# A hybrid diffusion step on one core: expert rows turned elsewhere, the choice of experts inside scoring, half of the early sums on VectorE

## The reference

```python
def peer_ffn(h, wq, subkeys, u_tab, v_tab):
    ...
        q = (xt @ wq).reshape(PEER_CHUNK, PEER_HEADS, 2, PEER_HALF)
        sc = jnp.einsum('thpd,hpnd->thpn', q, subkeys).astype(jnp.float32)
        s_top, i_top = lax.top_k(sc, PEER_TOPK)
        cand = (s_top[:, :, 0, :, None] + s_top[:, :, 1, None, :]).reshape(PEER_CHUNK, PEER_HEADS, PEER_TOPK * PEER_TOPK)
        cidx = (i_top[:, :, 0, :, None] * PEER_NKEYS + i_top[:, :, 1, None, :]).reshape(PEER_CHUNK, PEER_HEADS, PEER_TOPK * PEER_TOPK)
        f_s, f_i = lax.top_k(cand, PEER_TOPK)
        e = jnp.take_along_axis(cidx, f_i, axis=-1)
        g = jax.nn.softmax(f_s, axis=-1).astype(xt.dtype)
        act = jax.nn.gelu(jnp.einsum('thkd,td->thk', u_tab[e], xt))
        return jnp.einsum('thk,thkd->td', g * act, v_tab[e])
```

## Time and profile before

| | us |
|---|---|
| Median of 3 runs | 3889.42 (3873.55 to 3904.28) |
| The profiled execution: its time, its span | 3899.92, 3898.1 |
| begin | 142.6 |
| project, att p (layer 0) | 153.6, 32.7 |
| rwkv p (layers 0, 1) | 160.6, 158.5 |
| score p (layers 0, 1) | 84.9, 92.5 |
| choose (layers 0, 1) | 31.0, 37.8 |
| att s, rwkv s, output s, score s (layer 0) | 105.6, 268.4, 84.8, 113.8 |
| exp (layers 0, 1) | 778.0, 737.9 |
| PE, DVE, ACT, POOL busy | 73%, 52%, 29%, 42% |
| DMA | 318 GB/s over the span |

### The profile page before, as it was taken

The page is one execution under the profiler, slowest core; times in us unless marked ns, Lnnn a source line. Parts: engine busy times, 40 slices in busy tenths (PEclk is TensorE's granted clock), DMA queues, the critical chain, the costliest instruction groups (busy, mean ns, idle before and its releaser), DMA issues. The chain is left out here.

```text
span 3898.1 us, 41250 instructions
## 1 busy us (share of the span) xinstructions
PE 2855.5 (73%) x13182; PEld 1768.7 (45%) x13182; DVE 2010.4 (52%) x5134; ACT 1112.1 (29%) x3048; POOL 1652.5 (42%) x1598
## 2 busy tenths in 40 slices
PE   5685775599776788888758675866996857777775
PEld 3584664356554233333228565843664622222221
DVE  1113337577567744444552234566765695445555
ACT  2444432332231211111124444433223212111111
POOL 0000002455334777777720000043643367777774
PEclk7897966799888999999979797767997999999998
DMA  9896972578877999999979798765987589999997
GB/s 386 327 361 237 365 275 100 210 254 296 313 249 248 362 410 410 411 410 409 409 290 348 253 360 315 251 245 188 327 294 275 189 318 362 384 392 409 406 408 280
DMA packets 332008, 1241.14 MB, mean 318 GB/s; under 512 B 41098, under 2 KB 45834, under 8 KB 316434
## 3 DMA queue, kind: packets, MB, share of 16 engines
q0 software_dynamic: 221184, 805.40, 54.5%
q10 hardware_dynamic: 75616, 276.96, 19.1%
q1 hardware_dynamic: 34996, 156.14, 10.6%
HBM read 1095.72 MB, written 142.64 MB: 318 GB/s over the span
## 5 line engine op out<-in xcount | busy, mean ns | idle before, releaser
L461 PE MATMUL acc<-more,rows 128*128 128x512 f32 x1712 | 820.8, 612 | 192.1 <-ACT rows L447 179.6
L423 DVE CUSTOM_DVE_ANT_0 rows<-rows,fetch_h_tok 128x1024 f32<-128x1024 f32 x536 | 655.0, 1223 | 437.9 <-DMA rows<-u_rows,fetch_eid 435.4
L402 POOL DMA_INDIRECT rows<-u_rows,fetch_eid x536 | 560.3, 1045 | 302.0 <-issue 155.5
L409 POOL DMA_INDIRECT more<-in_v,fetch_eid x428 | 452.6, 1057 | 386.9 <-PE acc L461 288.4
L441 ACT ACTIVATE fetch_gel<-fetch_dot 128x1 f32<-128x1 f32 x768 | 155.5, 203 | 1607.7 <-DVE fetch_dot L423 1593.2
L461 PEld LDWEIGHTS acc<-more,rows 128*128 128x128 f32 x1712 | 305.2, 192 | 638.7 <-issue 386.5
L461 PE MATMUL acc<-extra,rows 128*128 128x512 f32 x928 | 447.1, 609 | 145.5 <-ACT rows L447 130.8
L423 DVE CUSTOM_DVE_ANT_0 extra<-extra,fetch_h_tok 128x1024 f32<-128x1024 f32 x232 | 284.2, 1225 | 297.3 <-DMA extra<-u_rows,fetch_eid 297.0
L315 PE MATMUL rows_bank<-ident,rows 128*128 128x128 f32 x2048 | 301.7, 296 | 133.6 <-ACT rows L330 128.0
L330 ACT COPY rows<-rows_bank 128x512 f32<-128x512 f32 x512 | 276.3, 589 | 285.4 <-DMA u_rows<-rows 167.3
L461 PEld LDWEIGHTS acc<-extra,rows 128*128 128x128 f32 x928 | 160.2, 189 | 427.0 <-DMA extra<-in_v,fetch_eid 271.0
(11 more groups left out here) (918 smaller groups left out, 3827.0 us busy)
## 6 DMA issues: line engine op xcount, KB each, us to landing
rows<-in_u ACTq DMA_DIRECT2D x256, 512.0 KB, 6.4
u_rows<-rows ACTq DMA_DIRECT2D x256, 512.0 KB, 6.3
ring<-in_w_ada SPq DMA_DIRECT2D x48, 1024.0 KB, 8.1
ring<-in_wq SPq DMA_DIRECT2D x32, 1024.0 KB, 7.0
ring<-in_w_in SPq DMA_DIRECT2D x20, 1024.0 KB, 8.5
ring<-in_w_out SPq DMA_DIRECT2D x16, 1024.0 KB, 9.1
rows<-u_rows,fetch_eid POOLq DMA_INDIRECT x536, 6.6
more<-in_v,fetch_eid POOLq DMA_INDIRECT x428, 6.6
```

The costliest lines, as they stand in the source:

```text
L402: c.nc.gpsimd.indirect_dma_start(f.u[b], None, u_rows, bass.IndirectOffsetOnAxis(f.eid[:, t, k:k + 1], 0)).then_inc(c.landed_u[b], 16)
L409: c.nc.gpsimd.indirect_dma_start(f.v[b], None, v_rows, bass.IndirectOffsetOnAxis(f.eid[:, t, k:k + 1], 0)).then_inc(c.landed_v[b], 16)
L423: V.tensor_tensor_reduce(u, u, f.h_tok[:, t, :], 1.0, 0.0, ALU.mult, ALU.add, f.dot[:, n:n + 1]).then_inc(f.dots, 1)
L461: ins = c.nc.tensor.matmul(f.acc[2 * t + h][:, :], f.diag[:, n % DIAGS, :], f.v[f.place[n]][:, 512 * h:512 * h + 512], start=(k == 0), sto ...
```

## The change

Five things are changed.

1. No rows are turned in begin. `Turns_of` is 4 for grams, 2 for chunks and 3 for scan in place of 2, 1 and 2, so rwkv p turns 60 rows in each layer (46 before), and all 128 are turned when score p ends. Before, layer 0 had 18 rows in begin, 11 in score p and none in choose; layer 1 had 16 in score p and 13 in choose. Now score p has 15 in both.
2. `select` takes a range of heads. For the prompt it runs inside score p behind every second piece, for two heads at a time; choose keeps the last store of the rows, the exponential and the shares.
3. Of the slots below 114, every odd one (57 per layer) is summed on DVE into `summed`. ACT makes no diagonal for it, PE no product, and POOL's wait for its V buffer is on the sum's semaphore `added`. finish adds `summed` to `acc` for tile 0, with one operation more.
4. Blocks end without GpSimd's drain, and `clear` clears ranges of semaphores.
5. In exp, SP issues b_ada and w_ada first, and `load_for_norm` only when the samples' experts are chosen, since `select` there uses its buffer.

```diff
+BESIDE = 114
 class Turns_of:
-    begin, project, scores, values, grams, level, chunks, scan, out, q = 1, 2, 1, 1, 2, 3, 1, 2, 2, 1
+    project, scores, values, grams, level, chunks, scan, out, q = 2, 1, 1, 2, 4, 1, 2, 3, 1
...
 def clear(nc, sems):
-    for s in sems:
-        nc.sync.sem_clear(s)
-    nc.all_engine_barrier()
+    numbers = sorted(s.num for s in sems)
+    start = numbers[0]
+    for n, after in zip(numbers, numbers[1:] + [None]):
+        if after != n + 1:
+            nc.sync.sem_clear(range(start, n + 1))
+            start = after
+    nc.all_engine_barrier(sem_only=True)
...
+    f.by_vector = [n < BESIDE and n % 2 == 1 for n in range(STEPS)]
+    f.rank = [sum(1 for m in range(n + 1) if f.by_vector[m] == f.by_vector[n]) for n in range(STEPS)]
...
-                pool.wait_ge(f.slot_done, f.before[n] + 1)
+                m = f.before[n]
+                pool.wait_ge(f.added if f.by_vector[m] else f.slot_done, f.rank[m])
...
+        n = step - LAG
+        if 0 <= n < STEPS and f.by_vector[n]:
+            dve.wait_ge(c.landed_v[f.place[n]], f.count[n])
+            dve.wait_ge(f.weighted, n + 1)
+            if f.rank[n] == 1:
+                V.tensor_scalar(f.summed[:, :], f.v[f.place[n]], f.w[:, n:n + 1], None, ALU.mult).then_inc(f.added, 1)
+            else:
+                dve.wait_ge(f.added, f.rank[n] - 1)
+                V.scalar_tensor_tensor(f.summed[:, :], f.v[f.place[n]], f.w[:, n:n + 1], f.summed[:, :], ALU.mult, ALU.add).then_inc(f.added, 1)
...
-        if 0 <= n < STEPS:
+        if 0 <= n < STEPS and not f.by_vector[n]:
             t, k = divmod(n, SLOTS_OF_TOKEN)
             pe.wait_ge(c.landed_v[f.place[n]], f.count[n])
-            pe.wait_ge(f.diag_done, n + 1)
+            pe.wait_ge(f.diag_done, f.rank[n])
...
                 for m in range(TILES, N_ADA // PAIR):
                     ada_pair_copy(c, s, act, rows, m)
-                    rows_act(c, act, PAIR * Turns_of.begin)
...
                     ada_pair_product(c, s, pe, rows, piece_full, m)
-                    if m >= TILES:
-                        rows_pe(c, pe, PAIR * Turns_of.begin)
...
-        with nc.Block() as block:
+        with nc.Block(no_gpsimd_drain=True) as block:
...
+TOGETHER = 2
...
+                    if q is PROMPT and (m + 1) % TOGETHER == 0:
+                        if m + 1 == TOGETHER:
+                            dve.wait_ge(f.iota_in, 16)
+                        select(c, link, 0, lambda: None, spares, pick, m + 1 - TOGETHER, m + 1)
...
-def select(c, link, t, between, spares, pick):
+def select(c, link, t, between, spares, pick, first=0, end=PH):
...
-                dve.wait_ge(f.iota_in, 16)
-                select(c, link, 0, lambda: None, spares, pick)
                 rest_of_shares(c, dve, link, 0)
...
-                load_for_norm(c, l, sp, c.late_in, late, 1, "ln2")
                 if not last:
                     sp.dma_start(rows_mod[0:1, :], dram["b_ada"][l + 1:l + 2]).then_inc(S["bias_in"], 16)
...
                         fill_slot(c, sp, l, AT_ADA + n)
+                sp.wait_ge(f.routed, 2 * TILES)
+                load_for_norm(c, l, sp, c.late_in, late, 1, "ln2")
...
+                        if t == 0:
+                            ins = nc.vector.tensor_tensor(part[:, t, cols], c.fetch.acc[h][:, :], c.fetch.summed[:, cols], ALU.add)
...
+                    if t == 0:
+                        link(nc.vector.tensor_tensor(part[:, t, :], part[:, t, :], gates[:, 0, :], ALU.mult))
```

More of the change, by code:

```diff
@@ L38 @@
 WINDOW = 120
+BESIDE = 114
 DIAGS = 8
 class Turns_of:
-    begin, project, scores, values, grams, level, chunks, scan, out, q = 1, 2, 1, 1, 2, 3, 1, 2, 2, 1
+    project, scores, values, grams, level, chunks, scan, out, q = 2, 1, 1, 2, 4, 1, 2, 3, 1
 class Fetches_of:
-    begin, project, scores, values, grams, level, chunks, scan, out, q = 0, 0, 2, 2, 2, 3, 2, 2, 4, 1
+    scores, values, grams, level, chunks, scan, out, q = 2, 2, 2, 3, 2, 2, 4, 1
 SLOTS = 4
@@ L1865, in select @@
     V.scalar_tensor_tensor(rows_of[:, :, 1, :], halves[:, :, 1, :], float(NK), oddf, ALU.mult, ALU.add)
-    tops = f.top[:, t, :, :].rearrange("p (h two) k -> p h two k", two=2)
-    half0, half1, long = tops[:, :, 0, :], tops[:, :, 1, :], [P, PH, SHORT, TOPK]
+    tops = f.top[:, t, 2 * first:2 * end, :].rearrange("p (h two) k -> p h two k", two=2)
+    half0, half1, long = tops[:, :, 0, :], tops[:, :, 1, :], [P, heads, SHORT, TOPK]
     V.tensor_tensor(cand[:, :, 0:LONG_ROWS].rearrange("p h (a b) -> p h a b", a=SHORT),
@@ L1877, in select @@
         part = slice(8 * r8, 8 * r8 + 8)
-        for h in range(PH):
+        for h in range(heads):
             ins = V.max(best[:, h, part], cand[:, h, :])
@@ L1889, in select @@
     flat = pos.rearrange("p h k -> p (h k)")
-    V.tensor_tensor(f.share[:, t, :].rearrange("p (h k) -> p h k", h=PH), best[:, :, :],
-                    best[:, :, 0:1].to_broadcast([P, PH, TOPK]), ALU.subtract).then_inc(f.exp_asked, 1)
+    ins = V.tensor_tensor(f.share[:, t, ours].rearrange("p (h k) -> p h k", h=heads), best[:, :, :],
+                    best[:, :, 0:1].to_broadcast([P, heads, TOPK]), ALU.subtract)
+    if end == PH:
+        ins.then_inc(f.exp_asked, 1)
     V.tensor_copy(posf[:, :], flat)
```

71 lines of the change are left out of this document (39 added, 32 removed).

## The result

The changed kernel takes 3922.46 us (median of 9 runs, 3910.35 to 3929.99), the kernel before 3888.45 in the same comparison (9 runs). The ratio is 1.0092, 95% interval 1.0066 to 1.0117. I had forecast 3838 us.

What follows compares the result with a forecast made beforehand. Limits were taken by stage: transfers in begin and mid rwkv p, PE in score p, DVE in choose. Terms -40.6 + 52 - 10 - 22 - 14 - 26 + 8.6 = -52 took 3889.4 to 3838 us; range 3785 to 3885.

Steps and rivals of the forecast that it cites:

- Part 5, sums: Slots summed on VectorE instead of PE, mainly in the levels of rwkv s: -13 us a layer, -26 in all.
- DVE takes PE's place, and 0.8 us a level are left: Solve level in rwkv s: PE's 10.51 us become 7.9, DVE needs 9.7, so 0.8 of 2.6 us is gained.
- Att s runs at POOL's pace: 0: In att s POOL sets the pace, so the sums there change nothing: 0 us.
- The slower rival: Sums land on the path, each adding its 1.225 us: +140 for -26, 4003 us; chance 8%.
- Part 2, rows: Fourteen more rows in each rwkv p at 1.85 us a row, between 15 and 36 us: +52 for two layers.
- Part 3, choice: Choice inside score p: 9.8 us per two heads, stage bound by DVE, 118 us with choose; sum -10.
- Part 4, boundaries: Between stages: fewer semaphore clears give -22 us, GpSimd's drain left out behind att s gives -14.
- A drain left out can't cost: Stage ends: leaving out GpSimd's drain gives -14 us, or 0 if the hole is another wait.
- Part 6, exp: Exp and finish: about 0 in exp of layer 0, +6 in layer 1, 1.3 a layer in finish; sum +8.6.
- The sign that I gave, no wait for b_ada: Exp of layer 0: as long as before, without PE's wait of 23 us for b_ada.
- The -12: Exp of layer 0: with b_ada loaded first, 12 us of transfers not moved at the start are regained.
- the full-price rows: Rival: rows at full price in rwkv p and a cold clock in score p: -16, 3873 us; chance 22%.

Runs made afterwards that it cites:

- bounds_only: Kernel before with only the boundaries changed (semaphore ranges cleared at once, no GpSimd drain, lighter barrier): ratio 0.9860 to the kernel before.
- bias_first: Kernel before with the cheap boundaries and b_ada loaded ahead of the norm's loads in exp: ratio 0.9853 to the kernel before.

## Why the prediction was wrong

In us of 3880, forecast against measured (by ratios): rows (with begin) +13, +46; choice -8, +3; boundaries -39, -54; sums with exp and finish -17, +36. The misses are +33, +11, -15 and +53, together 82 of the 84 us by which 3838 was too low. Each measured part is good to some 15 us, the choice to 20.

**Part 5, sums: the sign was wrong**, the largest miss. The step that failed is "DVE takes PE's place, and 0.8 us a level are left". I compared the two engines' work in a level, and took the larger for its period. But the level is a chain through DVE, ACT and PE, not two engines side by side: ACT's gelus, ahead of its copy for the level, wait for dots behind sums. The levels stayed at 10.5 us in the mean, 13.97 and 7.07 in turn, and 6 us a layer were lost in rwkv s ahead of them and behind. Just what holds the engines up there stays open. "Att s runs at POOL's pace: 0" failed too: with sums it is 3 to 6 us longer than without them (93.9 and 93.6 in bounds_only) in each kernel that has them on cheap boundaries. Score s takes 2 to 3 us more. The slower rival (each sum's 1.225 us on the path) had the mechanism right and the size too large: by the ratios sums cost 25 to 36 us, 0.2 to 0.3 a sum, where I had counted a gain of 0.23.

**Part 2, rows: the price and the place.** I took 1.85 us a row between 1.1 and 2.6; measured 2.8 to 3.2 in the levels and some 2.5 in output p. The upper bound, the full transfer, was in the rows that I showed (392 GB/s, share 1.01, not the 1.02 that I gave the rival), and I left it for a mean over the stage, partly because I had put the added rows where the transfers were slack, by misreading the table. Had I printed PE's order at a level, four groups of `rows` products in place of three would have shown it. Begin itself came out right: -37.7 for -40.6, its pairs 6.2 us apart for 6.1.

**Part 3, choice**: the 9.8 us a group, and in layer 0 the 112 us of score p and the 5.9 of choose, were right to 2%; layer 1's score p took 105.4. The base was not. The old score p, bound by PE, moves by 15 to 18 us with the clock, the new one by 11 (104.2 to 115.6 us, at 0.66 to 0.78), and a difference between the two can't be taken from one execution.

**Part 4, boundaries**: the mechanism was right, the size low. "A drain left out can't cost" was right and hid a condition: alone it gives nothing either.

**Part 6, exp**: "about 0" and +6 against +4.8 and -4.4 by the stage lengths; nothing decides on it. The sign that I gave, no wait for b_ada, failed: PE still waits 14.7 us for it in the changed kernel (12.0 in bias_first, 23.3 before). The -12 came, as -11.4, only in bias_first and the kernels built on it, where the norm's loads follow b_ada at once.

Of the rivals, the full-price rows came with the slower sums; I had them as exclusive, each beside a forecast that was otherwise right. My range held no case in which two went wrong together, and that is the case that came.
